# Layer norms by halves of the tokens: three closing units instead of two, and tiles of their own for the next stage's first weights

## What is computed

```python
def layer_norm(x, g, b):
    xf = x.astype(jnp.float32)
    mu = jnp.mean(xf, axis=-1, keepdims=True)
    var = jnp.mean(jnp.square(xf - mu), axis=-1, keepdims=True)
    return ((xf - mu) * lax.rsqrt(var + EPS) * g + b).astype(x.dtype)
...
        x = layer_norm(DEEPNORM_ALPHA * x + g1 * y, ln_g[l, 0], ln_b[l, 0])
        h = modulate(x, sh2, sc2)
        x = layer_norm(DEEPNORM_ALPHA * x + g2 * sq_relu_mlp(h, mlp_w1[l], mlp_w2[l]), ln_g[l, 1], ln_b[l, 1])
```

## Time and profile before

| | us |
|---|---|
| timed runs | 2582.86, 2585.76, 2589.31 |
| their median | 2585.76 |
| the profiled execution, its own time | 2583.25 |
| its span, first to last instruction | 2581.4 |
| TensorE busy | 2519.9 (98%) |
| vector engine busy | 1580.2 (61%) |
| ScalarE busy | 1047.8 (41%) |
| GpSimd busy | 271.3 (11%) |

### The profile page before, as it was taken

One profiled execution on the slowest core, in us unless ns is written; L12 is line 12 of the kernel. 1 busy time (PEld: TensorE's weight loads), 2 busy tenths in 40 slices (PEclk: granted clock), 3 DMA queues, 4 the chain that ended last, 5 costly groups with the idle time before them and its releaser, 6 DMA issues.

```text
span 2581.4 us, 37858 instructions
## 1 busy us (share of the span) xinstructions
PE 2519.9 (98%) x13134; PEld 2081.7 (81%) x13134; DVE 1580.2 (61%) x2525; ACT 1047.8 (41%) x1663; POOL 271.3 (11%) x187
## 2 busy tenths in 40 slices
PE   8999999999999999999999999999999999999997
PEld 6887788888887788888888866788888888888886
DVE  6763765656578866555575886655556765744445
ACT  5333622223357852222254277553223523622333
POOL 2320100000220010000031100400001302200003
PEclk9999999999999999999999999999999999999999
DMA  3221444444420034444442100244444343333222
GB/s 136 74 83 54 133 146 147 138 149 142 148 82 26 26 104 137 150 139 147 146 134 79 49 1 2 82 136 141 142 150 141 99 146 120 103 98 102 93 95 82
DMA packets 79340, 277.50 MB, mean 107 GB/s; under 512 B 8448, under 2 KB 11904, under 8 KB 78720
## 3 DMA queue, kind: packets, MB, share of 16 engines
q1 hardware_dynamic: 58560, 205.55, 24.3%
q10 hardware_dynamic: 20672, 70.51, 8.3%
HBM read 273.92 MB, written 2.10 MB: 107 GB/s over the span
## 4 chain that ended last, share of the span: by engine, by line
PE 87%; DVE 6%; ACT 4%; issue 1%; POOL 1%; DMA 1%; ACTq 0%; SPq 0%; DVEq 0%; POOLq 0%
PE banks L2459 67%; PE banks L2639 5%; PE banks L2503 2%; PE banks L3078 1%; PE banks L2952 1%; PE banks L2673 1%; PE banks L3020 1%; PE banks L2928 1%; PE banks L3049 1%; ACT attn_e L1291 1%; ACT norm_sq L1152 1%; PE banks L2913 1%; DVE w_lo L1415 1%; DVE attn_e L2324 1%; DVE nsa_e L1982 0%
## 5 line engine op out<-in xcount | busy, mean ns | idle before, releaser
L685 ACT ACTIVATE w_hi<-w_raw 128x1024 fp32r<-128x1024 f32 x362 | 381.3, 1053 | 641.0 <-PE banks L2459 532.1
L2459 PE MATMUL banks<-h_hi,w_hi 128*128 128x512 f32 x1536 | 602.3, 392 | 0.7 <-DVE w_lo L1415 0.7
L2459 PE MATMUL banks<-h_hi,w_lo 128*128 128x512 f32 x1536 | 597.9, 389 | 0.0
L2459 PE MATMUL banks<-h_lo,w_hi 128*128 128x512 f32 x1536 | 597.7, 389 | 0.0
L1415 DVE TENSOR_TENSOR w_lo<-w_raw,w_hi 128x1024 fp32r<-128x1024 f32 x362 | 453.5, 1253 | 97.7 <-ACT w_hi L685 81.8
L2459 PE MATMUL banks<-g_hi,w_hi 128*128 128x512 f32 (+1 forms) x1100 | 421.8, 383 | 1.6 <-DVE g_lo L2360 0.9
L2459 PE MATMUL banks<-g_hi,w_lo 128*128 128x512 f32 (+1 forms) x1100 | 419.5, 381 | 0.0
L2459 PE MATMUL banks<-g_lo,w_hi 128*128 128x512 f32 (+1 forms) x1100 | 419.5, 381 | 0.0
L2459 PEld LDWEIGHTS banks<-h_hi,w_hi 128*128 128x128 f32 x1536 | 288.4, 188 | 63.1 <-issue 1.7
L2459 PEld LDWEIGHTS banks<-h_lo,w_hi 128*128 128x128 f32 x1536 | 288.4, 188 | 60.7 <-issue 1.7
L2459 PEld LDWEIGHTS banks<-h_hi,w_lo 128*128 128x128 f32 x1536 | 288.3, 188 | 60.1
(11 more groups left out here) (445 smaller groups left out, 3461.6 us busy)
## 6 DMA issues: line engine op xcount, KB each, us to landing
w_raw<-weights SPq DMA_DIRECT2D x384, 512.0 KB, 3.3
ada_raw<-ada ACTq DMA_DIRECT2D x112, 512.0 KB, 3.3
nsa_bias<-nsa_bias ACTq DMA_DIRECT2D x6, 512.0 KB, 3.6
x<-x SPq DMA_DIRECT2D x4, 512.0 KB, 6.8
out<-x SPq DMA_DIRECT2D x8, 256.0 KB, 2.1
mix_cum<-ret_tab ACTq DMA_DIRECT2D x1, 1024.0 KB, 4.8
rows_c<-c_rows ACTq DMA_DIRECT2D x1, 1024.0 KB, 5.3
nsa_w<-cmp_w ACTq DMA_DIRECT2D x1, 1024.0 KB, 5.6
```

Of the source, the lines that this page charges most:

```text
L685: act.activation(w_hi[s][:], w_raw[s][:], ACT.Copy).then_inc(w_hi_done, 1)
L2459: mm = pe.matmul(bank, w[slot][:, k, :], m[:, k, :], start=(n == 0 and a == 0), stop=(n == kts - 1 and a == 2))
```

## The change

The half-wise part of a stage's end grows from the last two units to the last three. PE no longer runs the unit before (pair i - 1, s = 1) as a whole: it does the first half of three units, then the second half of three, in the slots 1, 0, 2 and the banks 1, 0, 7 (first) and 5, 6, 7 (second). Tiles 5, 6 and 7 of x are therefore taken by halves (`take(half, u)`, u = 0 to 2), squared by halves, and summed by halves on GpSimd. Since slot 1 stays in use until the end, the next stage's first unit gets a tile pair of its own, `opening_w_hi` and `opening_w_lo` (slot 5, `OPENING = (5, 3)`). On DVE, the split of the next stage's second weight goes from between two takes of half 0 to behind `normal(0, 0)` for r = 5 to 7 (it stood there already for r = 4), and `normal(0, 1)`, `centre(0, 2)`, `normal(0, 2)` go ahead of the last take. On ACT, `chunk(0, 3)` goes ahead of `root_half(1)`, and the split of the third weight behind `chunk(0, 0)`. In the opening, one group of the third unit's matmuls goes ahead of the sums of half 1. The number of loads, and of matmuls apart from those cut in two, is the same.

```diff
+        OPENING = (5, 3)
...
+        CLOSING_SLOTS, CLOSING_BANKS = (1, 0, 2), ((1, 0, 7), (5, 6, 7))
...
+            def half_norm(r):
+
+                centred_sums(r)
+                half_sums(r, 0, 0)
+                half_sums(r, 0, 1)
+                half_sums(r, 1, 0)
+                if r < 8:
+                    low_chunk(r, 0, 0)
+                half_sums(r, 1, 1)
+                if r < 8:
+                    for c in range(1, 2 * 4):
+                        low_chunk(r, c // 4, c % 4)
...
-                m = 2 * (PAIRS[name] - 2)
                 split_hi(i, 0)
-                body(i - 1, 0, m)
+                body(i - 1, 0, 2 * (PAIRS[name] - 2))
                 split_hi_to(2, i, 1, 2 * i - 1)
+                square(0, 0)
                 if more:
-                    split_hi_to(1, i + 1, 0, 2 * i)
-                body(i - 1, 1, m + 1)
-                if more and r > 4:
-                    split_hi_to(3, i + 1, 1, 2 * i)
-                square(0, 0)
+                    split_hi_to(OPENING[0], i + 1, 0, 2 * i - 1)
                 square(0, 1)
-                if r == 4:
-                    split_hi_to(3, i + 1, 1, 2 * i)
+                square(0, 2)
+                if more:
+                    split_hi_to(OPENING[1], i + 1, 1, 2 * i - 1)
                 root_half(0)
+                square(1, 0)
+                if more:
+                    act.wait_ge(aux_done, max(1, r - 4))
+                chunk(0, 0)
                 if more:
                     split_hi_to(0, i + 2, 0, 2 * i + 1)
                 if r == 4:
                     load_ctx()
-                square(1, 0)
+                square(1, 1)
+                chunk(0, 1)
+                square(1, 2)
+                chunk(0, 2)
                 if more:
-                    act.wait_ge(aux_done, max(1, r - 4))
-                    chunk(0, 0)
-                square(1, 1)
-                if not more:
-                    chunk(0, 0)
-                chunk(0, 1)
-                if more:
-                    chunk(0, 2)
+                    chunk(0, 3)
                 root_half(1)
...
-                m = 2 * (PAIRS[name] - 2)
                 split_lo(i - 1, 1)
-                body(i - 1, 0, m)
+                body(i - 1, 0, 2 * (PAIRS[name] - 2))
                 split_lo(i, 0)
                 split_lo_to(2, i, 1)
-                body(i - 1, 1, m + 1)
+                take(0, 0)
                 if more:
-                    split_lo_to(1, i + 1, 0)
-                take(0, 0)
-                if more and r > 4:
-                    split_lo_to(3, i + 1, 1)
+                    split_lo_to(OPENING[0], i + 1, 0)
                 take(0, 1)
+                take(0, 2)
                 close(0)
                 centre(0, 0)
                 variance(0)
                 scale(0)
                 take(1, 0)
                 normal(0, 0)
-                if r == 4:
-                    split_lo_to(3, i + 1, 1)
+                if more:
+                    split_lo_to(OPENING[1], i + 1, 1)
                 centre(0, 1)
+                normal(0, 1)
                 take(1, 1)
-                normal(0, 1)
-                close(1)
                 centre(0, 2)
                 normal(0, 2)
-                variance(1)
+                take(1, 2)
+                close(1)
                 centre(0, 3)
                 normal(0, 3)
+                variance(1)
                 scale(1)
...
-                for s in range(2):
-                    pe.wait_ge(w_lo_done, 2 * i + s + 1)
-                    pe.wait_ge(bank_free[s], i)
-                    half_steps(psum[s], 2 * s, 0, hi, lo, range(kts), kts).then_inc(unit_half, 1)
-                half_steps(psum[6], 0, 1, hi, lo, range(6 if kts == KT else 5), kts)
+                for u in range(3):
+                    pe.wait_ge(w_lo_done, 2 * i + u)
+                    if u < 2:
+                        pe.wait_ge(bank_free[(u + 1) % 2], i - 1 + u)
+                    steps(0, u, range(kts)).then_inc(unit_half, 1)
+                steps(1, 0, range(kts - 1))
                 sum_half(r, 0)
-                half_steps(psum[6], 0, 1, hi, lo, range(6 if kts == KT else 5, kts), kts).then_inc(unit_done, 1)
-                half_steps(psum[7], 2, 1, hi, lo, range(kts // 2), kts)
+                steps(1, 0, range(kts - 1, kts)).then_inc(unit_done, 1)
+                steps(1, 1, range(kts // 2))
                 spread_half(r, 0)
-                half_steps(psum[7], 2, 1, hi, lo, range(kts // 2, kts), kts).then_inc(unit_done, 1)
+                steps(1, 1, range(kts // 2, kts)).then_inc(unit_done, 1)
+                pe.wait_ge(bank_free[1], i + 1)
+                steps(1, 2, range(kts)).then_inc(unit_done, 1)
...
                 first_steps(0)
+                pe.wait_ge(w_hi_done, 2 * (p0 + 1) + 1)
+                third_high(0, 0)
                 sum_half(r, 1)
                 steps(0, 0, 1)
                 steps(0, 1, 1)
-                pe.wait_ge(w_hi_done, 2 * (p0 + 1) + 1)
-                third_high(0, 0)
                 third_high(0, 1)
                 spread_half(r, 1)
```

More of the change, by code:

```diff
@@ L538, in low_halves @@
-            def low_halves(r):
-                for half in range(2):
-                    for c in range(4):
-                        part = (slice(None), slice(2 * c, 2 * c + 2), half_cols(half))
-                        pool.wait_ge(y_hi, 4 * KT + halves_before(r, half, 4) + c + 1)
-                        pool.tensor_tensor(h_lo[part], N["sq"][part], h_hi[part].bitcast(F32), ALU.subtract)\
-                            .then_inc(h_ready, 1)
+                    both = [(N["xc"], N["s1"], xc_done, 5 * (r - 5), xc_half, 2 * (r - 5))] + both
@@ L2572, in steps @@
                     pe.wait_ge(h_ready, 4 * KT + halves_before(r, half, 4) + c + 1)
-                    mm = half_steps(psum[s], 1 + 2 * s, half, h_hi, h_lo, (2 * c, 2 * c + 1))
+                    mm = half_steps(psum[s], OPENING[s], half, h_hi, h_lo, (2 * c, 2 * c + 1))
                     if half == 1 and c == 3:
```

114 lines of the change are left out of this document (58 added, 56 removed).

## The result

| | before | after |
|---|---|---|
| median of 7 runs each | 2584.69 | **2593.20** |
| lowest to highest | 2582.86 to 2589.31 | 2592.11 to 2599.66 |
| profiled execution, its span | 2581.4 | 2591.4 |

All in us. The ratio is 1.0033, with a 95% interval of 1.0024 to 1.0043: the change makes the kernel slower by 8.5 us. The interval reaches 0.1% to either side, so the difference is clear of none. It leaves open on which side of 0.3% the difference lies, which the prediction had taken for the least that can be told.

What follows compares the result with a forecast made beforehand. The prediction took TensorE, busy for 98% of the span, as the bound. It summed 2.8 (r = 4) + 3 x 1.7 (r = 5 to 7) - 0.5 (r = 8) = 7.4 us onto 2585.76, giving 2593.2 us, range 2584.5 to 2599.

Steps and rivals of the forecast that it cites:

- The forecast: Whole kernel: slower by 5 to 9 us, point 2593.2 us, given a 50% chance.
- The opening's gap and the first half: r = 5: first norm_diag 1.8 us earlier; TensorE's 1.62 us gap at the opening gone.
- The new wait at the second sums: r = 5: TensorE newly waits 1.0 to 2.5 us for the second half's column sums.
- The two collisions: r = 5 to 7: GpSimd's h_lo delays the add and norm_diag; 1.7 us taken per norm, between 0 and 2.2.
- r = 4: Closing of ffn1_down2: second spread 2.1 to 3.1 us later through ScalarE's queue, taken as 2.8.
- So I work out r = 5 and take it three times: r = 5, 6 and 7 share code and have alike waits, so 3 x 1.7 us.
- Behind the spread ... the program is the same as before: Behind the second spread TensorE nearly never waits, so each us the spread is later is a us of the kernel.
- r = 8: Last closing, no weights to split and no h_lo: second spread 0.5 us earlier, between 1 earlier and 0.3 later.
- The narrower steps: Units cut in two: 0.013 us more per step, 1.5 us in all, not adding to the end in r = 4 to 7.
- theory B: Rival account set for the experiments: time is lost on TensorE itself, by narrower steps or the clock; no chance given.
- The waits for norm_s: Sign in the changed trace: TensorE's wait for column sums grows from 2.0 to 8 us or so, norm_diag's from 4.5 to about 7.
- The sum: Whole kernel: 2.8 + 3 x 1.7 - 0.5 = 7.4 us slower, 2593.2 us.

Runs made afterwards that it cites:

- e2: Changed kernel, GpSimd holding h_lo of the second chunk until the second half's sums are added, of the fourth until norm_diag is made; 2588.73 us, ratio 1.0012.
- e1: Changed kernel with ScalarE taking the second half's root ahead of the first half's fourth chunk again; 2589.96 us, ratio 1.0017 against the kernel before.
- after_again: The changed kernel, unedited, run once more for a second profile; 2595.31 us.
- e8: Kernel before with the three half-wise units at r = 8 alone; 2583.34 us, ratio 0.9994.
- e3: Changed kernel with the vector engine's split behind normal(0, 0) done twice for r = 5 to 7; 2601.59 us, ratio 1.0061 against the kernel before.
- e4: Changed kernel with e1's ScalarE order and the second half's last two takes, adds and variance ahead of the first half's chunks 2 and 3; 2603.32 us, ratio 1.0066.
- e5: Changed kernel with the edits of e1 and e2 together; 2587.31 us, ratio 1.0014 against the kernel before.
- e7: Changed kernel with the split for r = 5 to 7 back among the first half's takes, ScalarE's copy ahead of its third square; 2604.49 us, ratio 1.0076.
- e6: Kernel before with only the split of r = 5 to 7 moved behind normal(0, 0); 2585.94 us, ratio 1.0004.
- e9: Kernel before with three half-wise units at r = 8 alone and the split of r = 5 to 7 behind normal(0, 0); 2584.13 us, ratio 0.9993.

## Why the prediction was right, and where it was off

The forecast was the case that came: 2593.2, slower by 5 to 9 us. Its account holds for the mechanism; some terms were off and partly made up for each other.

**The opening's gap and the first half.** Right. The first sums of r = 5 came 1.82 us earlier (1.8 forecast for norm_diag, which hangs on them), and TensorE reached the opening without a wait for h_hi in all four.

**The new wait at the second sums.** Right: 2.02 us in r = 5, 6 and 7 (1.0 to 2.5 forecast).

**The two collisions.** Right, and now shown by e2: 1.45 and 1.22 us against the 0.42 and 0.43 that the same instructions take when h_lo is held back. I discounted them to 1.7 of 2.2 us for each norm, and the second spread came 1.71, 2.08 and 2.33 us later. In r = 5 the 1.71 is in part luck: both collisions struck in full, and the vector engine got from the first norm_diag to the add in 7.2 us (1665.27 to 1672.49), not in 7.6. The prediction also took the collisions for the whole loss. e1 leaves the first one in place, and the second spread is at 27.20 all the same. So no single term owns the 1.7 us: either edit alone takes them back in r = 5.

**r = 4.** Right: 2.63 us (2.8 forecast). The weights came 0.53 and 0.66 us late (0.7 and 0.5 forecast). e1 shows that 1.7 of the 2.63 are the chunk ahead of the root.

**"So I work out r = 5 and take it three times".** This step failed, by 0.4 and 0.6 us. The first sums had a small wait in r = 5 (0.55 us), but 0.92 in r = 6 and 1.18 in r = 7, because the raw weight of the next stage lands later behind their T0. ScalarE's copies in r = 6 and r = 7 after:

```profile
2017.61 1.06 ACT L707 ACTIVATE opening_w_hi<-w_raw 128x1024 fp32r<-128x1024 f32 x1 [0.62 <-DMA w_raw<-weights]
...
2205.05 1.06 ACT L707 ACTIVATE opening_w_hi<-w_raw 128x1024 fp32r<-128x1024 f32 x1 [0.91 <-DMA w_raw<-weights]
```

They start 7.2 and 7.5 us behind T0, against 6.6 in r = 5 after, where ScalarE doesn't wait for the load. With the first sums moved forward by 1.8 us, this load is the first thing in their way. For r = 7 the trace of before had it: its copy starts 7.3 us behind T0 there, and it cost nothing since the half-wise steps came later. For r = 6 it had not (6.5 us, as in r = 5); why that load lands later in the kernel after (7.2, 7.9 and 8.3 us in after, after_again and e1) stays open.

**"Behind the spread ... the program is the same as before".** This step failed too. In r = 5 the spread is 1.71 us later and the unit behind the opening 2.42, in r = 6 2.08 and 3.25, in r = 7 2.33 and 2.29. The 0.7 and 1.2 us extra are not a wait, they are matmuls at half the clock: r = 7 had no low stretch and none of this, nor had r = 5 in the second execution (28.95 to 42.97, 14.0 us as before). Each spread is 2.0 us later on the mean; the three norms together cost 8.0 us where I had 5.1.

**r = 8.** The direction was right, the size 1.30 us instead of 0.5: the spread came 0.75 us earlier and the end of the span 1.30. The 0.55 us behind the spread are the clock. The spread's matmuls, first before, then after:

```profile
2571.84 1.22 PE L2528 MATMUL banks<-norm_diag,tab 128*128 128x256 f32 x2 [2.70 <-DVE norm_diag L2128]
...
2582.33 0.70 PE L2536 MATMUL banks<-norm_diag,tab 128*128 128x256 f32 x2 [1.94 <-DVE norm_diag L2137]
```

In all 13 executions the clock falls to its lower level at the very end, from 21.6 to 25.1 us behind this T0; so the slices of "Time and profile before" were too coarse to say that it is at its full level throughout. In after it fell 0.6 us behind the spread's start (25.13), elsewhere mostly ahead of it. The second execution of after, where it fell at 22.93, takes 1.22 us for these matmuls again and 34.16 us to the end, as e8 does. So the change itself gives 0.6 to 0.8 us at r = 8, close to the forecast, and the rest of the 1.30 is luck.

**The narrower steps.** TensorE's busy time grew by 5.8 us, of which these steps would be some 1.5 by the prediction's own rows, and the low clock a part of the rest. As forecast, the steps add nothing to r = 4 to 7, since TensorE waits there anyway; theory B is right only for the clock. The waits for norm_s grew to 12.1 us (8 forecast) and those for norm_diag to 5.6 (7 forecast). The late load adds to the first. The low clock hides some of the second: in r = 5 TensorE waits 1.79 us for norm_diag at full clock (the second execution) and not at all at half.

**The sum.** Forecast 2.8 + 5.1 - 0.5 = 7.4; measured in the profiled pair 2.63 + 7.96 - 1.30 + 0.65 = 9.9, and in the medians 8.5. Some 1.9 us of the 9.9 are the low clock at r = 5 and 6, which the prediction didn't have. That the point came out within 0.1 us is luck, as the medians of before alone moved by 1 us from 3 to 7 runs.

## What to carry to other kernels

Giving TensorE more work ahead of a wait pays only as far as the queues behind that wait can use the head start: add up what each in-order queue has to do between the two places before moving anything. When one engine is given its input later, list which instruction of another engine it then overlaps with: the add of r = 5 began 0.10 us behind GpSimd's h_lo and was held for a whole us. A collision that is taken away can come back at the next instruction, as the 128x2 step of e2 and e5 shows, so read the whole chain again and not only the two rows that were changed. Where one repeated stage stands for several, look in each at the load that has slack, as that is what differs.

## What the runs showed of the hardware

**The clock fell beside half-wise norms.** TensorE's granted clock, 1.00 in before from T0 to the opening's end, fell to its lower level (1.2 GHz) for a few us in some norms. Two executions of the kernel after, r = 5: stretch in us, its length, busy us of PE, PEld, DVE, ACT and POOL (instructions), granted clock, DMA share, GB/s. The first:

```profile
1650.10:1673.97 23.87, 21.73 (x174) 20.99 (x172) 19.79 (x34) 12.86 (x22) 13.98 (x13) 1.00 0.31 103
...
1675.00:1682.00 7.00, 7.00 (x33) 6.82 (x33) 4.86 (x11) 2.85 (x6) 2.11 (x2) 0.52 0.00 1
```

The second:

```profile
1674.79:1679.88 5.09, 3.48 (x27) 3.23 (x27) 3.59 (x10) 2.42 (x5) 2.54 (x2) 1.00 0.00 0
1679.88:1693.90 14.02, 13.88 (x106) 13.21 (x107) 10.21 (x13) 10.07 (x18) 5.74 (x4) 1.00 0.23 76
```

Both stood 2.02 us until the second sums. The first ran the next 6.8 us or so at half the clock, and its half-width steps came 0.21 us apart instead of 0.12:

```profile
1680.53 0.41 PE L2511 MATMUL banks<-h_hi,opening_w_lo 128*128 128x256 f32 x1
1680.74 0.41 PE L2511 MATMUL banks<-h_hi,opening_w_hi 128*128 128x256 f32 x1
```

It went on at 43.72 behind T0, the second at 42.98: 0.7 us for the low stretch. Part of what the stretch takes is hidden: in the second run TensorE stands idle for 1.79 us before the spread, in the first not at all. Over the norms r = 4 to 7, low stretches stood at 2 and 3 of 4 in the two executions of after, at 2 in e1 and e2, and at all 4 in e3, e4, e5 and e7. In the five executions with two closing units at these norms there were none in both of before, in e6 and in e8, and 2 in e9. So the three half-wise units make them more frequent, but don't bring them alone: e6 and e9 run the same program at these norms, one execution with none and one with two. The length of the waits alone doesn't decide either: e5's are at most 1.4 us and it had four, e6 stands 1.6 us at each opening and had none. What does decide stays open. A similar stretch near 785 us, ahead of everything the change touches, lasted 3.4 to 17.1 us from run to run, in both kernels, and is part of their spread.

**A vector instruction with two operands in SBUF waits for GpSimd's to end, however small it is.** In e2 the 128x2 step of the variance ran from 1674.67 to 1675.86, where the second of two h_lo ended at 1675.85 (1673.33 + 2.52):

```profile
1673.33 2.52 POOL L554 TENSOR_TENSOR h_lo<-norm_sq,h_hi 128x512 fp32r<-128x512 f32 x2 [1.71 <-DVE norm_s L2120]
```

In e6 the same 128x2 step ended at 1674.98, h_lo at 1674.96. The step before it, which reads one operand, from PSUM, took 0.16 us in the middle of that h_lo (1673.70 to 1674.96):

```profile
1673.90 0.16 DVE L2116 TENSOR_SCALAR norm_st<-banks 128x4 f32<-128x4 f32 x1
```

The page "SBUF — State Buffer" of the Trainium skill (🔬 SBUF: two separate sides) says that of a vector instruction with two SBUF inputs and a GpSimd one that reads SBUF, whichever starts first keeps the ports to its end. These rows agree, to 0.02 us. For 256 columns the loser ends 0.3 us behind the holder (it takes 0.42 alone), and for 2 columns 0.02 us behind (0.16 alone). So the loser's time is the rest of the holder's plus its own less some 0.14 us, in both sizes. I had priced the two large instructions this way, and not the small ones.
